# A decoder trunk with product-key experts: 16 tokens of the dense part scored by fetched rows

## The chip, the cores and the metric

One core of one Trainium2 chip runs the whole kernel. The metric is the device time of one execution in microseconds; the number quoted is the median of several runs. The profile and the trace come from one more execution, which has its own time.

## What is computed

One layer of a hybrid decoder for 512 tokens of width 1024: a parallel attention block (sliding-window attention and native sparse attention, merged by gates), a PEER expert layer, a gated per-layer embedding, and a last RMSNorm. The change lies in the PEER layer:

```python
def peer(h, w_q, sub_k1, sub_k2, u, v):        # 16384 experts, 8 heads x 16 picks a token
    ...
    sc, pos = lax.top_k(cand, PEER_TOPK)
    eidx = jnp.take_along_axis(cidx, pos, axis=-1)
    gate = jax.nn.softmax(sc, axis=-1)
    ...
    def chunk_fn(args):
        hx, ex, gx = args
        act = jax.nn.gelu(jnp.einsum('td,thkd->thk', hx, u[ex]))
        return jnp.einsum('thk,thkd->td', (gx.astype(act.dtype) * act), v[ex])
```

Each token picks 128 experts. For each of them the token's row is multiplied with the expert's row of `u`, put through a gelu, weighted by a gate, and used as the weight of the expert's row of `v`.

## The kernel before

The 512 tokens are four tiles of 128. Attention and projections fill the first 540 us. Then the PEER layer is computed in two ways at once.

**Tiles 0 and 1, by fetched rows.** GpSimd issues an indirect DMA per pick (`gather`, L549): it brings, for all 128 tokens of a tile, each token's own row of 1024 floats, 512 KB in all, into one of 8 slots. The `u` rows (n = 0 to 255) are multiplied with the tokens by VectorE (`dot`, L1252, the operation at L1257), then the `v` rows (n = 256 to 511) are weighted and added up (`sum_early`, L1269, and `accumulate`, L1280, the operation at L1292). A fetch waits until the row 8 before it is used (`row_used`), and every consumer waits until its row has landed.

**Tiles 2 and 3, densely, on TensorE.** All 16384 experts go through as 128 chunks of 128. For chunk c, eight matmuls (L1753, 256 token columns each; fp32, so that a matmul is two passes in the trace) give the scores of 256 tokens; ScalarE puts them through the gelu (`dense_activate`, L796). The gates are turned into a matrix of the same shape, four tokens at a time, as a product of two one-hots: `make_hots` on VectorE (L1338), `part_hots` and `gate_hots` on ScalarE (L815, L824), and `mix` on TensorE (L1732, four matmuls of 128 columns). There are 64 such groups, one after each of the score chunks 62 to 125. ScalarE copies the part of a group's product for the chunks still to come (`copy_mix`, L808), VectorE multiplies the chunks already there (`apply_mix`, L1301), and for later chunks it multiplies the gelu with the copied part (`apply_late`, L1309). When the 128 score chunks are done, 128 value chunks follow (`values`, L1764; the operation at L1766), each of four matmuls of 512 columns. The blocks of `u` and `v`, 512 KB a chunk, are streamed by SyncE through a ring of four.

**Who waits for whom.** The orders are written out by hand:

- VectorE takes 134 rows (`EARLY_DOTS`), with the expert search of tiles 1 to 3 between them, then makes the first one-hots. Then there are 65 steps of one-hots, late product, mix product and 2, 2 or 3 rows (`STEP_ROWS`), 151 rows in all. After them the rest of tile 0's `v` rows, then 128 rows of tile 1 with the tail's parts at fixed row numbers (L1396 to L1419).
- TensorE turns the picks of tiles 2 and 3 before chunk 60 (`turn_picks`, L1720). It needs the first one-hots after chunk 62. The tail of tile 0 (the layer embedding and last norm) is placed among the value chunks: `tail_turn(0)` before chunk 80 needs the closed sum of tile 0, and `tail_gate(0)` before chunk 100 (`FIRST_TAIL + 20`, L1774) needs the operand that VectorE makes in `tail_turned(0)` (L1177), placed after its row 42 of tile 1.
- VectorE adds the dense sums of tiles 2 and 3 (`add_dense`, L1220) after its rows 102 and 103 of tile 1. The first waits for tile 2's last value chunk, the second for tile 3's. TensorE's tails of tiles 2 and 3 follow, and the tail of tile 1 comes last, after `close(1)` (L1294).

```python
                if k == 42:
                    tail_turned(0)
                ...
                if c == FIRST_TAIL + 20:
                    tail_gate(0)
                    tail_embed(0)
```

Of the kernel before, what the change touches and what calls it, by code (L numbers as in the profile page):

```python
# [74 lines left out]
EARLY_DOTS = 134  # L75
STEP_ROWS = (2, 2, 3)
# [26 lines left out]
def build(nc, a, out):  # L103
# [4 lines left out]
    with ctx:  # L108
# [14 lines left out]
        pkeys = small[:, 312:568].rearrange("p (h n) -> p h n", h=2)  # L123
        eidx = sb("eidx", [P, NG * COLS], i32)
# [36 lines left out]
        mix_rows = sum(STEP_ROWS[s % len(STEP_ROWS)] for s in range(WG + 1))  # L161
        early_sums = EARLY_DOTS + mix_rows - NG * COLS
        low_slots = NG * COLS + -(-early_sums // SLOTS) * SLOTS
# [79 lines left out]
        assert ha == XS + NG * D  # L243

# [17 lines left out]
        def chunk_scores(c):  # L262
            return ps[6 + c % 2][:, 0:DT]
# [7 lines left out]
        def first_copied(g):  # L271
            return FIRST_MIX + g + 1
# [61 lines left out]
        experts_known = sem("experts_known")  # L334
        row_gathered = [sem(f"row_gathered{b}") for b in range(SLOTS)]
# [191 lines left out]
        def _(pool):  # L527
# [20 lines left out]

            def gather(n):  # L549
                values, k = divmod(n, NG * COLS)  # L550
# [13 lines left out]
                if n >= SLOTS:  # L564
                    pool.wait_ge(row_used, n - SLOTS + 1)
                if low_slots <= n < low_slots + SLOTS and n % SLOTS >= SLOTS - 2:
                    pool.wait_ge(dense_scores, CHUNKS)
                G.indirect_dma_start(out=row_slot(n), out_offset=None, in_=a["v"] if values else a["u"],  # L568
                                     in_offset=bass.IndirectOffsetOnAxis(ap=eidx[:, col:col + 1], axis=0)
                                     ).then_inc(row_gathered[n % SLOTS], 16)  # L570
# [33 lines left out]
            for n in range(2 * NG * COLS):  # L604
                gather(n)
                for t in range(1, TILES):
# [10 lines left out]
        def _(act):  # L617
# [174 lines left out]
            def gelu_dots(t):  # L792
                act.wait_ge(row_used, COLS * (t + 1))
                A.activation(dots[:, t, :], dots[:, t, :], ACT.Gelu_apprx_tanh).then_inc(gelu_ready, 1)

            def dense_activate(c):  # L796
                late = WGRP * groups_before(c)
# [6 lines left out]
                if late < DT:  # L804
                    last = A.activation(mixed[:, c, late:DT], sc[:, late:DT], ACT.Gelu_apprx_tanh)  # L805
# [18 lines left out]
            def gate_hots(g):  # L824
                act.wait_ge(hot2_apart, g + 1)
                for j in range(WGRP):
                    tok = WGRP * g + j
                    last = A.activation(hot2[:, g % 2, j, :], hot2[:, g % 2, j, :], ACT.Relu,  # L828
                                        scale=pickT[:, 3, tok:tok + 1], bias=pickT[:, 2, tok:tok + 1])
                last.then_inc(hot2_gated, 1)  # L830

            for c in range(CHUNKS):
                if c == 8:
                    act.wait_ge(experts_known, 3)
                if c == TURN_AT:
                    act.wait_ge(picks_turned, 2)
# [11 lines left out]
                dense_activate(c)  # L848
                if 0 <= g + 1 < WG:
                    gate_hots(g + 1)  # L850
                if c == 40:
                    gate_exp(2)
# [19 lines left out]
        def _(dve):  # L872
# [379 lines left out]
            def dot(t, k):  # L1252

                n = t * COLS + k
# [14 lines left out]
            def sum_early(k):  # L1269

                n = NG * COLS + k
# [8 lines left out]
            def accumulate(t, k):  # L1280

                n = (NG + t) * COLS + k
# [11 lines left out]
            def close(t):  # L1294
                dve.wait_ge(row_used, (NG + t + 1) * COLS)
# [12 lines left out]

            def apply_late(c):  # L1309
                late = WGRP * groups_before(c)  # L1310
                if late == 0:
                    return
                dve.wait_ge(dense_gelu, c + 1)
                dve.wait_ge(mix_copied, groups_before(c))
                V.tensor_tensor(mixed[:, c, 0:late], mixed[:, c, 0:late], late_gelu[:, c % LATE, 0:late],  # L1315
                                ALU.mult).then_inc(late_applied, 1)
# [21 lines left out]
            def make_hots(g):  # L1338
                if g >= 2:
                    dve.wait_ge(mix_made, g - 1)  # L1340
                V.tensor_tensor(hot1[:, g % 2, :, :], iota[:, :].unsqueeze(1).broadcast_to([P, WGRP, P]),
# [6 lines left out]
            for k in range(EARLY_DOTS):  # L1348
# [15 lines left out]
                if k == EARLY_DOTS - 13:  # L1364
                    gates(2)
                    gates(3)
            def take_row(n):
                if n < NG * COLS:
                    dot(*divmod(n, COLS))
                    return  # L1370
                if n == NG * COLS:
                    weigh(0)
                sum_early(n - NG * COLS)
# [15 lines left out]
            for c in range(FIRST_MIX + WG, CHUNKS):  # L1389
                apply_late(c)  # L1390
# [5 lines left out]
            for k in range(COLS):  # L1396
# [32 lines left out]
        def _(pe):  # L1429
# [290 lines left out]
            def turn_picks():  # L1720
# [9 lines left out]
                last.then_inc(picks_turned, 1)  # L1730

            def mix(g):  # L1732
                pe.wait_ge(hot1_ready, g + 1)
                pe.wait_ge(hot2_gated, g + 1)
                if g < 2:
                    pe.wait_ge(picks_out, 3)
                else:
                    pe.wait_ge(mix_applied, g - 1)
# [133 lines left out]
```

## Time and profile before

| | |
|---|---|
| median of 3 runs | 1641.18 us (1641.04 to 1641.79) |
| the profiled execution, time | 1641.71 us |
| the profiled execution, span of the trace | 1639.9 us |
| TensorE, matmuls | 1608.1 us busy (98%) |
| TensorE, weight loads | 1044.2 us (64%) |
| VectorE | 1043.8 us (64%) |
| GpSimd | 667.2 us (41%) |
| ScalarE | 430.9 us (26%) |
| DMA | 477.70 MB, mean 291 GB/s over the span |
| granted TensorE clock, mean | 0.996 |

The span is the stretch that the trace covers; the time has 1.8 us more around it. Busy time is the time in which an engine has an instruction under way. The granted clock is a share of TensorE's full 2.4 GHz. In the rows, PE is TensorE's matmuls, PEld its weight loads, DVE is VectorE, ACT ScalarE, POOL GpSimd; "arena" is the one large buffer in which most tiles lie, so names tell little and the line numbers count. A bracket behind a timeline row is the idle time before it and who ended it.

### The profile page before, as it was taken

To read this page: it belongs to the slowest core of one execution; us is meant where nothing else is said; L and a number is where in the kernel's file an instruction comes from. 1 tells how busy PE (TensorE), PEld (TensorE's weight loads), DVE (VectorE), ACT (ScalarE), POOL (GpSimd) and SP (SyncE) were. 2 spreads that over 40 slices of the span, in tenths; PEclk is the share of its full clock that TensorE was granted. 3 is DMA by queue.
4 is the path that set the end of the run, shared out by engine and by line. 5 is a ranking of instruction groups with operands and counts; after the bars stand their busy time and mean duration, and the time that the engine had idled before them with its cause. 6 is when DMAs were issued, how large, how long until landed. Compare 5 with 4: busy or idle time off the path is not lost.

```text
span 1639.9 us, 18326 instructions
## 1 busy us (share of the span) xinstructions
PE 1608.1 (98%) x6294; PEld 1044.2 (64%) x6294; DVE 1043.8 (64%) x2380; ACT 430.9 (26%) x1262; POOL 667.2 (41%) x707
## 2 busy tenths in 40 slices
PE   7999999999999999999999999999999999999997
PEld 4446444446786688888899999995444444444443
DVE  2012444432269999999878999996555566667465
ACT  2003444350110211111167777760000000000013
POOL 0002445540001474466745555555433345456340
PEclk9999999999999999999999999999999999999999
DMA  6224111105435899999999999999999999999962
GB/s 232 85 79 148 44 39 39 39 27 167 144 140 175 316 378 401 391 402 397 402 409 408 405 400 408 404 389 406 409 409 409 410 409 406 409 409 409 400 205 91
DMA packets 132698, 477.70 MB, mean 291 GB/s; under 512 B 14796, under 2 KB 15820, under 8 KB 132605
## 3 DMA queue, kind: packets, MB, share of 16 engines
q0 software_dynamic: 73728, 268.47, 41.6%
q1 hardware_dynamic: 58876, 208.06, 34.1%
q8 instruction: 50, 0.82, 0.2%
q14 instruction: 44, 0.35, 0.1%
HBM read 472.24 MB, written 4.24 MB: 291 GB/s over the span
## 4 chain that ended last, share of the span: by engine, by line
PE 93%; DVE 2%; issue 1%; ACT 1%; DMA 1%; POOL 1%; DVEq 0%; SPq 0%
PE psum L1753 27%; PE psum L1766 26%; PE psum L1653 7%; PE psum L1578 6%; PE psum L1454 5%; PE psum L1740 3%; PE psum L1602 3%; PE psum L1614 3%; PE psum L1538 2%; PE psum L1696 2%; PE psum L1553 2%; PE psum L1524 1%; PE psum L1470 1%; PE psum L1638 1%; PE psum L1489 1%
## 5 line engine op out<-in xcount | busy, mean ns | idle before, releaser
L1753 PE MATMUL psum<-arena 128*128 128x256 f32 x2048 | 453.4, 380 | 1.7 <-ACT arena L721 1.7
L1766 PE MATMUL psum<-arena 128*128 128x512 f32 x1024 | 440.3, 593 | 1.7 <-DVE arena L1315 1.1
L1753 PEld LDWEIGHTS psum<-arena 128*128 128x128 f32 x2048 | 384.5, 190 | 51.1 <-issue 2.2
L568 POOL DMA_INDIRECT arena<-in_u,eidx x256 | 257.8, 1007 | 382.7 <-DVE arena L1023 168.2
L568 POOL DMA_INDIRECT arena<-in_v,eidx x256 | 262.2, 1024 | 293.7 <-DVE arena L1292 171.2
L1766 PEld LDWEIGHTS psum<-arena 128*128 128x128 f32 x1024 | 194.6, 190 | 246.1 <-issue 241.3
L1257 DVE CUSTOM_DVE_ANT_0 arena<-psum,arena 128x1024 f32<-128x1024 f32 x256 | 299.9, 1220 | 11.8 <-DMA arena<-in_u,eidx 11.2
L1292 DVE SCALAR_TENSOR_TENSOR arena<-arena,wts 128x1024 f32<-128x1024 f32 x175 | 222.7, 1287 | 106.2 <-DMA arena<-in_v,eidx 106.1
L544 POOL TENSOR_SCALAR arena<-arena 128x256 f32<-128x256 f32 (+4 forms) x128 | 105.9, 846 | 251.3 <-DVE arena L977 191.5
L1578 PE MATMUL psum<-arena 128*128 128x512 f32 x256 | 118.4, 606 | 0.0
L1653 PE MATMUL psum<-arena 128*128 128x256 f32 x512 | 114.7, 384 | 2.4 <-ACT arena L710 2.4
L1653 PEld LDWEIGHTS psum<-arena 128*128 128x128 f32 x512 | 97.6, 193 | 15.8 <-ACT arena L710 3.0
L828 ACT ACTIVATE arena<-arena 128x128 f32<-128x128 f32 x256 | 105.0, 488 | 0.0
L1292 DVE SCALAR_TENSOR_TENSOR psum<-arena,wts,psum 128x1024 f32<-128x1024 f32 x50 | 64.4, 1289 | 49.8 <-DMA arena<-in_v,eidx 49.8
L1454 PE MATMUL psum<-arena 128*128 128x512 f32 x208 | 89.8, 593 | 0.2 <-ACT arena L648 0.2
L805 ACT ACTIVATE arena<-psum 128x256 f32<-128x256 f32 (+31 forms) x126 | 41.3, 328 | 177.3 <-PE psum L1753 176.9
L739 ACT ACTIVATE arena<-arena 128x1024 f32<-128x1024 f32 x4 | 4.2, 1059 | 311.3 <-PE psum L1766 248.0
L820 ACT ACTIVATE arena<-iota,arena 128x128 f32<-128x128 f32 x256 | 81.4, 396 | 0.0
L1578 PEld LDWEIGHTS psum<-arena 128*128 128x128 f32 x256 | 46.1, 190 | 55.4 <-issue 54.4
L686 ACT ACTIVATE arena<-arena 128x256 f32<-128x256 f32 (+4 forms) x128 | 59.8, 469 | 55.2 <-DVE arena L964 44.0
L1454 PEld LDWEIGHTS psum<-arena 128*128 128x128 f32 x208 | 39.4, 190 | 49.3 <-issue 48.6
L1740 PEld LDWEIGHTS psum<-arena 128*128 128x128 f32 x512 | 67.3, 192 | 3.2
(195 smaller groups left out, 1419.8 us busy)
## 6 DMA issues: line engine op xcount, KB each, us to landing
arena<-in_ut SPq DMA_DIRECT2D x128, 512.0 KB, 6.7
arena<-in_vd SPq DMA_DIRECT2D x128, 512.0 KB, 6.9
arena<-in_wpack SPq DMA_DIRECT2D x105, 512.0 KB, 3.6
arena<-in_u,eidx POOLq DMA_INDIRECT x256, 8.8
arena<-in_v,eidx POOLq DMA_INDIRECT x256, 14.7
arena<-in_w_pg SPq DMA_DIRECT2D x8, 512.0 KB, 9.2
arena<-in_x SPq DMA_DIRECT2D x4, 512.0 KB, 5.0
arena<-bias_rows SPq DMA_DIRECT2D x8, 256.0 KB, 5.7
```

Of the source, the lines that this page charges most:

```text
L544: last = G.tensor_scalar(sw[:, i % 3, r, 0:w], sw[:, i % 3, r, 0:w], scl[:, i, r:r + 1], None, ALU.mult)
L568: G.indirect_dma_start(out=row_slot(n), out_offset=None, in_=a["v"] if values else a["u"], in_offset=bass.IndirectOffsetOnAxis(ap=eidx[:, ...
L820: last = A.activation(hot2[:, g % 2, j, :], iota[:, :], ACT.Abs, scale=-1.0, bias=pickT[:, 1, tok:tok + 1])
L828: last = A.activation(hot2[:, g % 2, j, :], hot2[:, g % 2, j, :], ACT.Relu, scale=pickT[:, 3, tok:tok + 1], bias=pickT[:, 2, tok:tok + 1])
L1257: V.tensor_tensor_reduce(out=row_slot(n), in0=dot_rows[t], in1=row_slot(n), scale=1.0, scalar=0.0, op0=ALU.mult, op1=ALU.add, accum_out=do ...
L1292: V.scalar_tensor_tensor(to, row, w, to, ALU.mult, ALU.add).then_inc(row_used, 1)
L1454: last = T.matmul(ps[j % 8], blk(j)[:, k * P:(k + 1) * P], hT[:, k, :], start=(k == 0), stop=(k == KC - 1))
L1578: last = T.matmul(ps[4], blk(B_MG + m)[:, k * P:(k + 1) * P], hT[:, k, :], start=(k == 0), stop=(k == KC - 1))
L1653: last = T.matmul(ps[4 + p % 2][:, jj * HT:(jj + 1) * HT], blk(b)[:, k * P:(k + 1) * P], h2T[:, k, :], start=(k == 0), stop=(k == KC - 1))
L1740: last = T.matmul(mix_bank(g)[:, j * P:(j + 1) * P], hot1[:, g % 2, j, :], hot2[:, g % 2, j, :], start=True, stop=True)
L1753: last = T.matmul(chunk_scores(c), u[:, k * P:(k + 1) * P], h2T1[:, k, :], start=(k == 0), stop=(k == KC - 1))
L1766: last = T.matmul(ps[VALUE_BANK[t] + h], mixed[:, c, t * P:(t + 1) * P], stream[:, c % SRING, h * HALF:(h + 1) * HALF], start=(c == 0), st ...
```

## The change

The last 16 tokens of tile 3 leave the dense scores, which then have 240 columns. Their 128 picks each are spread over the 128 partitions as 8 parts of 16 picks (16 tokens x 8 parts), so that 16 more fetched `u` rows serve all of them (n = 176 to 191). TensorE makes the spread token rows with matmuls against an identity (`mid_rows`) and the spread picks and gates with two more matmuls; VectorE makes the dot products (`mid_dot`), ScalarE the gelu, and the weights are turned back by one small matmul in chunk 98. For the last four groups the weight is multiplied into the first one-hot, and the mix product is copied whole, with no gelu to multiply it with. Besides, `apply_late` goes from VectorE's queue to GpSimd's, between the fetches; VectorE takes 136 early rows and then 2, 2, 2, 2 or 3 a step; and the dense tiles are added ten rows earlier.

```diff
-EARLY_DOTS = 134
-STEP_ROWS = (2, 2, 3)
+EARLY_DOTS = 136
+STEP_ROWS = (2, 2, 2, 2, 3)
+MID = 16
+MID_PARTS = P // MID
+MID_AT = 176
+MID_GELU = FIRST_MIX + 30
+MID_BACK = FIRST_MIX + 36
+DN = DT - MID
+MID_FIRST = DN // WGRP
...
+        u_rows = NG * COLS + MID
+        early_sums = rows_taken(WG + 1) - u_rows
...
         def chunk_scores(c):
-            return ps[6 + c % 2][:, 0:DT]
+            return ps[6 + c % 2][:, 0:DN]
...
-            for n in range(2 * NG * COLS):
+            def apply_late(c):
+                late = WGRP * late_groups(c)
+                if late == 0:
+                    return
+                pool.wait_ge(dense_gelu, c + 1)
+                pool.wait_ge(mix_copied, late_groups(c))
+                G.tensor_tensor(mixed[:, c, 0:late], mixed[:, c, 0:late], late_gelu[:, c % LATE, 0:late],
+                                ALU.mult).then_inc(late_applied, 1)
+
+            for n in range(2 * NG * COLS + MID):
                 gather(n)
+                for step in range(1, WG + 1):
+                    if n == rows_taken(step) + SLOTS - 1:
+                        apply_late(FIRST_MIX + step - 1)
+                        if step == WG:
+                            for c in range(FIRST_MIX + WG, CHUNKS):
+                                apply_late(c)
...
+            def widen():
+                act.wait_ge(rows_stashed, 16 * TILES)
+                A.activation(token_wide.rearrange("p (q c) -> p q c", c=MID),
+                             ident[:, P - MID:P].unsqueeze(1).broadcast_to([P, MID_PARTS, MID]), ACT.Copy).then_inc(mid_wide_ready, 1)
+                for k in range(KC):
+                    last = A.activation(h_wide[k // 4][:, k % 4, :].rearrange("p (q c) -> p q c", c=MID),
+                                        h2T1[:, k, DN:DT].unsqueeze(1).broadcast_to([P, MID_PARTS, MID]), ACT.Copy)
...
             for c in range(CHUNKS):
+                if c == 48:
+                    widen()
...
             make_hots(0)
+            spread_picks()
             taken = EARLY_DOTS
             for s in range(WG + 1):
-                if s + 1 < WG:
+                if 1 <= s < WG - 1:
                     make_hots(s + 1)
-                if s >= 1:
-                    apply_late(FIRST_MIX + s - 1)
+                if 1 <= s <= MID_FIRST:
                     apply_mix(s - 1)
+                if s == MID_GELU - FIRST_MIX + 3:
+                    weigh_mid()
                 more = STEP_ROWS[s % len(STEP_ROWS)]
                 for n in range(taken, taken + more):
                     take_row(n)
                 taken += more
-            for c in range(FIRST_MIX + WG, CHUNKS):
-                apply_late(c)
+                if s == 0:
+                    dve.wait_ge(mid_rows_made, 1)
+                    make_hots(1)
+            dve.wait_ge(mix_copied, WG)
...
-                if k == 102:
+                if k == 92:
                     add_dense(2)
-                if k == 103:
+                if k == 93:
                     add_dense(3)
                     tail_scale(1)
-                if k == 105:
+                if k == 95:
                     tail_turned(1)
                     tail_scale(2)
-                if k == 106:
+                if k == 96:
                     tail_turned(2)
...
+                pe.wait_ge(mid_wide_ready, 3)
+                T.matmul(ps[5][:, DT:DT + P], token_wide, esel.rearrange("p h k -> p (h k)"), start=True, stop=True)
+                T.matmul(ps[5][:, DT + P:DT + 2 * P], token_wide, gateD[:, 1, :], start=True,
+                         stop=True).then_inc(picks_turned, 1)
+
+            def mid_rows():
+                pe.wait_ge(row_used, COLS)
+                for k in range(KC):
+                    last = T.matmul(ps[k // 4][:, (k % 4) * P:(k % 4 + 1) * P],
+                                    h_wide[k // 4][:, k % 4, :], ident[:, :], start=True, stop=True)
+                last.then_inc(mid_rows_made, 1)
...
                 for k in range(KC):
-                    last = T.matmul(chunk_scores(c), u[:, k * P:(k + 1) * P], h2T1[:, k, :], start=(k == 0), stop=(k == KC - 1))
+                    last = T.matmul(chunk_scores(c), u[:, k * P:(k + 1) * P], h2T1[:, k, 0:DN], start=(k == 0), stop=(k == KC - 1))
+                if c == MID_BACK:
+                    pe.wait_ge(mid_weighed, 1)
+                    last = T.matmul(ps[6 + c % 2][:, DT:DT + MID], mid_wide, mid_same_token, start=True, stop=True)
                 last.then_inc(dense_scores, 1)
+                if c == TURN_AT + 1:
+                    mid_rows()
```

The new reductions on VectorE, right behind the first one-hots:

```diff
+            def spread_picks():
+                apart = [P, 2, MID_PARTS, MID]
+                V.tensor_reduce(mid_same_part, ident[:, :].rearrange("p (q c) -> p q c", c=MID), AX.X, ALU.add)
+                after(V.tensor_reduce(mid_same_token, ident[:, :].rearrange("p (q c) -> p c q", c=MID), AX.X, ALU.add))
+                V.tensor_tensor(mid_pick.rearrange("p a (q c) -> p a q c", c=MID),
+                                ps[5][:, DT:2 * DT].rearrange("p (a q c) -> p a q c", a=2, c=MID),
+                                mid_same_part.unsqueeze(1).unsqueeze(3).broadcast_to(apart), ALU.mult).then_inc(mid_spread, 1)
```

## Rows read from the trace of the kernel before

**Rows 1.** The chain that ended last, shares by engine.

```profile
PE 93%; DVE 2%; issue 1%; ACT 1%; DMA 1%; POOL 1%; DVEq 0%; SPq 0%
```

**Rows 2.** Windows by stage: us, busy us (count) per engine, clock, DMA share, GB/s.

```profile
617.00:833.00 216.00, 215.23 (x1001) 189.72 (x1002) 197.82 (x618) 38.34 (x90) 127.06 (x141) 1.00 1.01 399
833.00:1114.00 281.00, 281.00 (x1550) 254.51 (x1549) 259.03 (x460) 208.10 (x693) 151.78 (x149) 1.00 1.02 402
1116.00:1545.00 429.00, 428.43 (x1005) 190.23 (x1004) 264.08 (x213) 8.11 (x11) 206.71 (x202) 1.00 1.03 409
```

**Rows 3.** The chain in order of time: start us, us, engine, line, count.

```profile
548.05 15.77 PE psum L1653 x64
564.71 6.91 PE psum L1653 x32
617.77 204.05 PE psum L1753 x944
...
822.48 10.36 PE psum L1753 x48
833.73 3.46 PE psum L1753 x16
...
1107.57 6.92 PE psum L1753 x32
1115.61 268.05 PE psum L1766 x624
...
1460.90 13.73 PE psum L1696 x32
```

**Rows 4.** VectorE's waits from 612 to 830 us: us, times, longest.

```profile
DVE arena L1257 <- DMA arena<-in_u,eidx: 9.8, 10, 2.7
```

**Rows 5.** Timeline of VectorE before the mix: start us, us, instruction, idle before.

```profile
825.26 1.23 DVE L1257 CUSTOM_DVE_ANT_0 arena<-psum,arena 128x1024 f32<-128x1024 f32 x1 [1.54 <-DMA arena<-in_u,eidx]
826.41 1.29 DVE L1341 TENSOR_TENSOR arena<-iota,arena 128x512 f32<-128x512 f32 x2
...
833.77 0.69 DVE L1341 TENSOR_TENSOR arena<-iota,arena 128x512 f32<-128x512 f32 x1 [3.65 <-PE psum L1740]
```

**Rows 6.** Timeline of TensorE around 544 us.

```profile
543.66 1.06 PE L1627 MATMUL psum<-ident,arena 128*128 128x128 f32 x8 [2.27 <-DVE arena L1036]
```

**Rows 7.** Window of 2 us behind that gap, columns as in rows 2.

```profile
546.00:548.00 2.00, 1.18 (x6) 0.77 (x4) 1.93 (x3) 2.00 (x4) 0.00 (x0) 0.50 0.73 297
```

**Rows 8.** Timeline of VectorE late in the mix stage.

```profile
1109.74 0.41 DVE L1315 TENSOR_TENSOR arena<-arena,late_gelu 128x252 f32<-128x252 f32 x1
1110.07 0.67 DVE L1306 TENSOR_TENSOR arena<-arena,psum 128x504 f32<-128x504 f32 x1
1110.66 2.67 DVE L1278 SCALAR_TENSOR_TENSOR psum<-arena,wts,psum 128x1024 f32<-128x1024 f32 x2
```

**Rows 9.** Lines 601 and 1128: ns min/median/max, first and last start us.

```profile
L601 POOL TENSOR_TENSOR arena<-arena x18: 1443/1745/1762, 576.0 to 794.1; 128x800 f32<-128x800 f32 x12, 128x640 f32<-128x640 f32 x6
L1128 DVE TENSOR_TENSOR arena<-candno,arena x18: 818/992/2510, 574.2 to 786.5; 128x800 f32<-128x800 f32 x12, 128x640 f32<-128x640 f32 x6
```

**Rows 10.** Timeline of VectorE: turn of tile 0, and the end.

```profile
1430.59 1.28 DVE L1180 TENSOR_TENSOR arena<-psum,small 128x512 f32<-128x512 f32 x2
...
1543.27 1.29 DVE L1292 SCALAR_TENSOR_TENSOR arena<-arena,wts 128x1024 f32<-128x1024 f32 x1 [1.45 <-DMA arena<-in_v,eidx]
1567.44 1.28 DVE L1228 TENSOR_TENSOR arena<-arena,psum 128x512 f32<-128x512 f32 x2 [22.89 <-PE psum L1766]
...
1574.24 1.29 DVE L1228 TENSOR_TENSOR arena<-arena,psum 128x512 f32<-128x512 f32 x2 [4.32 <-PE psum L1766]
...
1581.76 16.04 DVE L1292 SCALAR_TENSOR_TENSOR arena<-arena,wts 128x1024 f32<-128x1024 f32 x13
...
1611.28 1.23 DVE L1299 TENSOR_TENSOR arena<-arena 128x1024 f32<-128x1024 f32 x1
```

**Rows 11.** Timeline of TensorE: tail gates of tiles 2 and 3.

```profile
1582.65 27.63 PE L1696 MATMUL psum<-arena 128*128 128x512 f32 x64
```

More of the change, by code:

```diff
@@ L160, in build, with rows_taken, u_row @@
         assert SL + (SLOTS - 2) * D <= XS
-        mix_rows = sum(STEP_ROWS[s % len(STEP_ROWS)] for s in range(WG + 1))
-        early_sums = EARLY_DOTS + mix_rows - NG * COLS
-        low_slots = NG * COLS + -(-early_sums // SLOTS) * SLOTS
+        def rows_taken(step):
+            return EARLY_DOTS + sum(STEP_ROWS[s % len(STEP_ROWS)] for s in range(step))
+        u_rows = NG * COLS + MID
+        early_sums = rows_taken(WG + 1) - u_rows
+        low_slots = u_rows + -(-early_sums // SLOTS) * SLOTS
+        def u_row(i):
+            return i if i < MID_AT else i + MID
         vslots = slots[:SLOTS - 2] + [place(H2 + i * D, [D])[0] for i in range(2)]
@@ L334, in build @@
         experts_known = sem("experts_known")
+        mid_wide_ready = sem("mid_wide_ready")
+        mid_spread = sem("mid_spread")
+        mid_known = sem("mid_known")
+        mid_rows_made = sem("mid_rows_made")
+        mid_gelu = sem("mid_gelu")
+        mid_weighed = sem("mid_weighed")
+        mid_weights_out = sem("mid_weights_out")
         row_gathered = [sem(f"row_gathered{b}") for b in range(SLOTS)]
@@ L546, in _, with fetch @@
                 last.then_inc(probs_ready, 1)
-            def gather(n):
-                values, k = divmod(n, NG * COLS)
+            def fetch(n, table, picks):
+                if n >= SLOTS:
+                    pool.wait_ge(row_used, n - SLOTS + 1)
+                if low_slots <= n < low_slots + SLOTS and n % SLOTS >= SLOTS - 2:
+                    pool.wait_ge(dense_scores, CHUNKS)
+                G.indirect_dma_start(out=row_slot(n), out_offset=None, in_=table,
+                                     in_offset=bass.IndirectOffsetOnAxis(ap=picks, axis=0)
+                                     ).then_inc(row_gathered[n % SLOTS], 16)
+            def gather(n):
+                if MID_AT <= n < MID_AT + MID:
+                    c = n - MID_AT
+                    if c == 0:
+                        pool.wait_ge(mid_known, 1)
+                    fetch(n, a["u"], mid_idx[:, c:c + 1])
+                    return
+                values, k = divmod(n - MID if n >= MID_AT else n, NG * COLS)
                 col = k // COLS * COLS + PICK_ORDER[k % COLS]
@@ L563, in gather @@
                     pool.wait_ge(rows_normed, 2 * TILES)
[L564 to L570, printed above, removed]
+                fetch(n, a["v"] if values else a["u"], eidx[:, col:col + 1])
             def number_pairs(t):
@@ L803, in dense_activate @@
                     last = A.activation(late_gelu[:, c % LATE, 0:late], sc[:, 0:late], ACT.Gelu_apprx_tanh)
-                if late < DT:
-                    last = A.activation(mixed[:, c, late:DT], sc[:, late:DT], ACT.Gelu_apprx_tanh)
+                if late < DN:
+                    last = A.activation(mixed[:, c, late:DN], sc[:, late:DN], ACT.Gelu_apprx_tanh)
                 last.then_inc(dense_gelu, 1)
@@ L1340, in make_hots @@
                     dve.wait_ge(mix_made, g - 1)
+                if g >= MID_FIRST:
+                    dve.wait_ge(mid_weights_out, 1)
+                    for j in range(WGRP):
+                        tok = WGRP * g + j
+                        last = V.tensor_scalar(hot1[:, g % 2, j, :], iota[:, :], pickT[:, 0, tok:tok + 1],
+                                               pickT[:, 2, tok:tok + 1], ALU.is_equal, ALU.mult)
+                    last.then_inc(hot1_ready, 1)
+                    return
                 V.tensor_tensor(hot1[:, g % 2, :, :], iota[:, :].unsqueeze(1).broadcast_to([P, WGRP, P]),
@@ L1736, in mix @@
                     pe.wait_ge(picks_out, 3)
+                    pe.wait_ge(mid_spread, 1)
+                elif g - 2 < MID_FIRST:
+                    pe.wait_ge(mix_applied, g - 1)
                 else:
-                    pe.wait_ge(mix_applied, g - 1)
+                    pe.wait_ge(mix_copied, g - 1)
                 for j in range(WGRP):
```

82 lines of the change are left out of this document (59 added, 23 removed).

## The prediction, made before the result

> **What bounds the kernel now.** I read the chain that ended last first: TensorE holds 93% of it, the dense scores (L1753) and the dense values (L1766) over half [rows 1]. Then the windows by stage [rows 2]: TensorE is busy throughout from 617 us on, but the DMA column matters as much. It stands at 399 GB/s beside the first scores, at 402 in the mix stage and at 409, its ceiling here, beside the values. So two flows run side by side: TensorE, and the fetched rows that VectorE consumes at the DMA's pace. Wherever TensorE waits for a row, the second flow sets the time.
>
> TensorE's steps [rows 3]: a score chunk takes 3.457 us (16 passes of 256 columns, 0.216 us each); a mix step is 4.347 us, so its four matmuls (8 passes of 128 columns) add 0.89 us, 0.111 us a pass. The scores end at 1114.5, the values begin at 1115.6, and at 1460.9 TensorE goes into the first tail gate (L1696), which follows value chunk 99.
>
> **Part 1: 240 columns in place of 256.** Between 0.111 us at 128 columns and 0.216 us at 256, a straight line gives 0.203 us at 240: 0.21 us less per chunk, 27 us over 128 chunks. The lower bound of the gain is zero, if the weight loads hold the pace; I take the line, since the loads already keep up with 0.111 us a pass in the mix. The new TensorE work before the mix, eight matmuls for the wide rows and two for the picks (20 passes of 128 columns), is 2.2 us; the back-turn of the weights is under 0.1 us. ScalarE's nine widening copies lie beside chunks in which it is used 38 us of 216 [rows 2]: nothing.
>
> **Part 2: before the mix, 62 chunks, 13 us of that gain.** TensorE would be ready for the first mix at 832.8 - 13.0 + 2.2 = 822. But this mix needs the first one-hots, which VectorE makes only after its early dots. Their last rows came late from the DMA: VectorE waited 9.8 us for rows in this stage [rows 4], 1.54 us just before the last early dot at 825.3, and made the one-hots at 826.4 [rows 5]. Now there are two more early dots (136), the streamed blocks come 6% faster and take that from the rows, and the new reductions stand ahead of the mix. VectorE's own work would let it be there at about 818 (826.4 less its waits, plus 2.3); the DMA's supply says 829 to 832 for the last row, then 0.7 us of one-hots and 1 us of spreading. I take 832.0 for the first mix, near the DMA's end, as the stage already moved 399 of 409 GB/s. So TensorE idles about 10 us there, and **12 of the 13 us are gone**. It also comes back slow: after the 2.27 us gap before 543.7 [rows 6] the granted clock fell to 0.50, the lower level (1.2 GHz) [rows 7], and 64 passes took 15.77 us where 32 take 6.91 soon after [rows 3]: 2.0 us lost.
> The Trainium skill, page "TensorE: Matmul & The Clock Gate" (section "What's actually happening"), has an idle array throttled to half rate; by that, too, the idle time costs more than itself. The trace agrees (0.50).
>
> **Part 3: the mix stage, 65 chunks.** TensorE gains 65 x 0.21 = 13.7 us. VectorE has per step one-hots 0.6, the mix product up to 0.67, and now 2.2 rows at 1.15 (dots) or 1.33 (sums) [rows 5, 8], 3.8 us with dots, under the new step of 4.14. Its late products (0.41 at 252 wide [rows 8]) go to GpSimd: by the 640-wide product there, 1.44 us [rows 9], some 0.6 us each, three of them at the end with 0.3 us more before the values. GpSimd is used 152 of 281 us [rows 2], so they fit; they wait for a chunk's gelu and mix copy, and behind them in the same queue stand the row fetches, which have 8 slots of lead. The DMA needs 512 KB per 4.14 us of stream and 2.2 rows: 406 GB/s, just under 409. So the scores end at 1114.5 - 0.8 - 13.7 + 2.0 = 1102.0 and the values begin at 1103.4, **12 us earlier**.
>
> **Part 4: the debt of rows.** By the end of the mix VectorE had taken 134 + 151 = 285 rows; now it has taken 136 + 143 = 279, 16 of which are new. So 22 more rows are left for the values stage. Which wait ends last there? The first tail gate needs the turned tile 0, and VectorE turns it after row 42 of tile 1 (L1400), a place the change leaves alone. Before, that was done at 1431.9 [rows 10], 29 us ahead of TensorE (1460.9). From 1113.3 [rows 8] it took 142 rows; now it must take 121 + 43 = 164. At 409 GB/s a 512 KB row costs 1.28 us, and a streamed block every 3.43 us leaves one row per 2.04 us: 22 rows are 45 us. From about 1100, the turn comes at 1100 + 317 + 45 = 1462, while TensorE is at chunk 100 at 1103.4 + 345.3 = 1448.7. Once TensorE stands and its four blocks are in, rows come at 1.28 us, which saves 2.5; the two turning operations add 1.3. So **TensorE stands about 12 us, until 1461**, and again loses 2.0 us to the low clock. The values end at 1461 + (1574.2 - 1460.9) + 2.0 = 1576.3: 2 us later than before. The bounds of this term: 4 us with the rows 10 us earlier (all the DMA's idle share before 1114 used), 18 us with the rows at the mix's old pace.
>
> **Part 5: the end.** The dense tiles are added at rows 92 and 93 in place of 102 and 103. VectorE already sat 22.9 us before the first of them, waiting for the values [rows 10]; at row 92 it sits there again, about 16 us by the same row count. After the values, 34 rows are left and not 24. From 1574.2 to 1612.4 VectorE is busy without a gap with 24 rows and the tail's parts [rows 10]; 13 rows take 16.04 us with their overlap, 1.19 each beyond the first, so ten more are 11.9 us: 50.1 us. They were covered once by TensorE's tail for tiles 2 and 3 (done at 1610.3, 2.3 us before tile 1's [rows 11]); the cover is used up, so all of it counts. Tile 1's tail stays 27.5 us, plus 0.7 (my estimate, a third of the 2.0 above) for a TensorE that now comes back from a longer idle time.
>
> **Sum**, against the profiled execution (span 1639.9, time 1641.7, so 1.8 around it): 1576.3 + 50.1 + 27.5 + 0.7 = 1654.6, and 1.8 makes 1656.4. The median shown is 0.5 lower: **1656 us**, 0.9% slower.
>
> **Rivals.**
> A (the forecast, 0.66): TensorE waits for row 42. Bounds 1643 to 1664.
> B (faster, 0.12): the rows keep up; neither wait arises, since gathers find unused DMA time and VectorE's own work ends by 818. Then 27 - 2.5 = 24.5 us stay: values end at 1549.7, and + 50.1 + 27.5 + 0.7 + 1.8 gives 1630. It decides if row 42's turn is done by 1437, 24 us ahead of my count. Against it: 409 GB/s at every window from 1116 on.
> C (no change, 0.10): the wait before the mix arises, that at the first tail gate doesn't (turn done by 1449): values end at 1562, total 1642. For it: the slack was 29 us; against it, 22 rows are 45 us.
> D (slower still, 0.12): the mix stage does not shrink, from either of two causes with one price: 240 columns save nothing, or GpSimd's products hold up VectorE. The trace has such a case: the 800-wide comparison on VectorE takes 0.99 us alone and up to 2.51 beside GpSimd's products [rows 9]. If a product of 0.6 us were added whole to VectorE's 3.8, its step would be 4.4, past 4.14. All 13.7 us would be lost: 1670. Against it: VectorE gives up its own late product.
> The Trainium skill, page "SBUF — State Buffer" (section "SBUF: two separate sides"), has VectorE operations with two SBUF inputs and GpSimd operations that read SBUF block each other whole; by it D's second cause holds for the one-hots, and the times of that comparison agree (0.99 and 2.51). The early dots read one input from PSUM, so by that rule they go free.
>
> **Numbers.** 0.2% (3.3 us) is about what a measurement of this kernel can tell from no change. Faster is B and a sliver of A, 0.13; same is C and A's edge, 0.11; slower 0.76. The range goes from 1641, which takes in C's 1642 and leaves out B, to 1668, short of D's full price.
>
> **What would show it.** Per step: a score chunk at 3.25 us on the chain; TensorE idle some 10 us before the first mix product, released by VectorE, with a granted clock of 0.5 behind it; the mix steps at 4.14; 279 rows taken when the values begin at about 1103; TensorE idle some 12 us before the first L1696 matmul, released by the turn of tile 0; VectorE idle before the dense add at row 92; 50 us from the last value to the last sum; GpSimd's products under 0.8 us. The forecast is wrong if the turn comes before TensorE asks for it, which needs rows faster than one per 2.04 us beside the stream, or if over 279 rows are taken by then; and its size is wrong if the mix steps stay at 4.35.

## The result and the profile after

The changed kernel takes **1662.4 us** (median of 4 runs, 1660.0 to 1663.2), beside 1641.1 (1637.4 to 1641.8) for the kernel before: 1.0132 times as long, interval 1.0113 to 1.0151. The forecast was 1656, with 1641 to 1668 as its range. On another chip the same file gave 1.0118 (1.0103 to 1.0134). The profiled execution took 1661.7 us, span 1659.9, so the same 1.8 us lie around it, and the sum of the prediction (span 1654.6) stands against 1659.9.

First the windows of the changed kernel, columns as in [rows 2]:

```profile
617.00:833.00 216.00, 204.44 (x1018) 191.08 (x1018) 199.37 (x617) 41.20 (x103) 126.88 (x142) 0.99 1.02 403
833.00:1114.00 281.00, 277.67 (x1572) 259.94 (x1573) 249.96 (x431) 204.94 (x688) 179.32 (x213) 0.99 1.02 403
1116.00:1545.00 429.00, 415.06 (x967) 183.62 (x966) 268.27 (x215) 8.11 (x11) 202.38 (x207) 0.98 1.03 409
```

TensorE, busy throughout before [rows 2], now has holes: 12 us in the first window, 14 in the last. The DMA is at 403 and 409 GB/s, where it was at 399 and 409: it was full, and it is full. What ended TensorE's holes is in its list of waits (us in total, times, longest):

```profile
PE psum L1798 <- DVE arena L1378: 14.7, 1, 14.7
PE psum L1807 <- DVE arena L1259: 13.6, 1, 13.6
PE psum L1865 <- DVE small L1449: 9.3, 1, 9.3
...
PE psum L1835 <- DVE arena L1243: 3.5, 1, 3.5
```

All four are releases by VectorE. The last two lie before the mix: `turn_picks` (L1835) waits for the dense gates and the first mix product (L1865) for the new reductions (L1449). The second is the first tail gate (L1807) waiting for the turned tile 0 (L1259). The first is tile 1's own turn, after the last row, where nothing else is left for TensorE.

Where the stages stand in TensorE's time (chain of waits; start us, us, line, count), as in [rows 3]:

```profile
834.89 2.04 PE psum L1865 x8
836.94 4.00 PE psum L1878 x16
840.94 0.89 PE psum L1865 x8
845.07 0.89 PE psum L1865 x8
```

The mix begins at 834.9. Its first eight passes take 2.04 us where later ones take 0.89, and the first chunk behind them 4.00 against 3.24: about 1.9 us lost to the low clock (a granted clock of 0.50 until 838.3 us, 1.00 from there on). From then on a step is 4.13 us (840.94 to 845.07), against 4.35 before [rows 3]. The other end, the turn of tile 0 in VectorE's timeline, and then TensorE's (start us, us, instruction, idle before):

```profile
1463.46 1.28 DVE L1259 TENSOR_TENSOR arena<-psum,small 128x512 f32<-128x512 f32 x2
```

```profile
1464.88 16.42 PE L1807 MATMUL psum<-arena 128*128 128x512 f32 x32 [13.57 <-DVE arena L1259]
1481.14 3.60 PE L1823 MATMUL psum<-arena 128*128 128x512 f32 x8
1484.58 96.30 PE L1897 MATMUL psum<-arena 128*128 128x512 f32 x224
1580.71 3.60 PE L1823 MATMUL psum<-arena 128*128 128x512 f32 x8
```

TensorE came to this gate at 1451.3, 9.6 us earlier than before (1460.9 [rows 3]), stood 13.57 us, and took 16.42 us for the 32 matmuls that took 13.73 (at a granted clock of 0.50 until 1469.8). So it left the gate 6.7 us later than before (1481.1, where it was 1474.5), and the value matmuls end 6.7 us later too. VectorE's timeline after them:

```profile
1574.11 1.29 DVE L1307 TENSOR_TENSOR arena<-arena,psum 128x512 f32<-128x512 f32 x2 [24.71 <-PE psum L1897]
...
1580.91 1.28 DVE L1307 TENSOR_TENSOR arena<-arena,psum 128x512 f32<-128x512 f32 x2 [4.32 <-PE psum L1897]
...
1588.43 28.44 DVE L1371 SCALAR_TENSOR_TENSOR arena<-arena,wts 128x1024 f32<-128x1024 f32 x23
...
1630.36 1.22 DVE L1378 TENSOR_TENSOR arena<-arena 128x1024 f32<-128x1024 f32 x1
```

VectorE sits 24.7 us at row 92 for the dense sums, and then has 23 rows in one block where it had 13 [rows 10]. From the second dense sum to the end of tile 1's sum (1580.9 to 1631.5) it takes 50.6 us, against 38.2 before.

### The profile page after: what moved, and what is told of

It is laid out like the page before. It is cut to its first block, busy times and chain, and to the rows that moved or that the text cites. A ratio compares the mean times of both kernels' runs of the same rounds, so it can differ in the third digit from the quotient of the medians.

```text
span 1659.9 us, 18445 instructions
## 1 busy us (share of the span) xinstructions
PE 1589.3 (96%) x6316; PEld 1048.2 (63%) x6316; DVE 1057.0 (64%) x2362; ACT 430.2 (26%) x1269; POOL 701.8 (42%) x788
## 2 busy tenths in 40 slices
DMA packets 135001, 486.09 MB, mean 293 GB/s; under 512 B 15051, under 2 KB 16075, under 8 KB 134908
## 4 chain that ended last, share of the span: by engine, by line
PE 53%; DMA 24%; DVE 14%; issue 4%; POOL 4%; ACT 1%; DVEq 0%; SPq 0%; POOLq 0%
DMA arena<-in_v,eidx 19%; PE psum L1878 11%; PE psum L1689 6%; PE psum L1897 6%; PE psum L1565 5%; DVE arena L1336 5%; DMA arena<-in_u,eidx 4%; PE psum L1764 3%; PE psum L1713 3%; PE psum L1725 3%; PE psum L1865 3%; PE psum L1649 2%; PE psum L1807 2%; POOL arena L587 2%; PE psum L1664 2%
## 5 line engine op out<-in xcount | busy, mean ns | idle before, releaser
L1878 PE MATMUL psum<-arena 128*128 128x240 f32 x2048 | 427.2, 367 | 1.7 <-ACT arena L778 1.7
L1878 PEld LDWEIGHTS psum<-arena 128*128 128x128 f32 x2048 | 384.5, 190 | 26.4 <-issue 2.4
L587 POOL DMA_INDIRECT arena<-in_v,eidx x256 | 252.6, 987 | 279.4 <-DVE arena L1371 173.6
L1897 PEld LDWEIGHTS psum<-arena 128*128 128x128 f32 x1024 | 194.3, 190 | 246.4 <-issue 243.5
L1371 DVE SCALAR_TENSOR_TENSOR arena<-arena,wts 128x1024 f32<-128x1024 f32 x186 | 236.1, 1290 | 110.3 <-DMA arena<-in_v,eidx 110.2
L1764 PE MATMUL psum<-arena 128*128 128x256 f32 x512 | 114.8, 383 | 2.4 <-ACT arena L767 2.4
L1371 DVE SCALAR_TENSOR_TENSOR psum<-arena,wts,psum 128x1024 f32<-128x1024 f32 x61 | 78.6, 1289 | 56.0 <-DMA arena<-in_v,eidx 55.9
L1764 PEld LDWEIGHTS psum<-arena 128*128 128x128 f32 x512 | 97.4, 193 | 16.0 <-ACT arena L767 3.0
L886 ACT ACTIVATE arena<-arena 128x128 f32<-128x128 f32 x240 | 98.4, 488 | 1.4 <-PE psum L1850 1.4
L862 ACT ACTIVATE arena<-psum 128x240 f32<-128x240 f32 (+29 forms) x122 | 39.0, 320 | 163.4 <-PE psum L1878 163.3
L1689 PEld LDWEIGHTS psum<-arena 128*128 128x128 f32 x256 | 46.0, 189 | 55.5 <-issue 54.4
L1865 PE MATMUL psum<-arena 128*128 128x128 f32 x512 | 68.5, 277 | 9.3 <-DVE small L1449 9.3
L1865 PEld LDWEIGHTS psum<-arena 128*128 128x128 f32 x512 | 67.9, 194 | 11.2 <-issue 9.6
## 6 DMA issues: line engine op xcount, KB each, us to landing
arena<-in_v,eidx POOLq DMA_INDIRECT x256, 14.7
```

Source lines behind the costliest of these rows:

```text
L587: G.indirect_dma_start(out=row_slot(n), out_offset=None, in_=table, in_offset=bass.IndirectOffsetOnAxis(ap=picks, axis=0)).then_inc(row_ga ...
L1371: V.scalar_tensor_tensor(to, row, w, to, ALU.mult, ALU.add).then_inc(row_used, 1)
L1689: last = T.matmul(ps[4], blk(B_MG + m)[:, k * P:(k + 1) * P], hT[:, k, :], start=(k == 0), stop=(k == KC - 1))
L1764: last = T.matmul(ps[4 + p % 2][:, jj * HT:(jj + 1) * HT], blk(b)[:, k * P:(k + 1) * P], h2T[:, k, :], start=(k == 0), stop=(k == KC - 1))
L1865: last = T.matmul(mix_bank(g)[:, j * P:(j + 1) * P], hot1[:, g % 2, j, :], hot2[:, g % 2, j, :], start=True, stop=True)
L1878: last = T.matmul(chunk_scores(c), u[:, k * P:(k + 1) * P], h2T1[:, k, 0:DN], start=(k == 0), stop=(k == KC - 1))
```

## The experiments

Twelve runs on four more chips, numbered 2 to 5 here. The kernel before was timed on each. The chips are of two kinds. On chips 4 and 5 it takes 1641.5 and 1641.2 us, as on the first chip. On chips 2 and 3 it takes 1652.0 and 1650.7, and on them the change costs much more, in a way told below. So ratios are compared only between chips of one kind. One more variant, with 128 early dots in place of 136, gave no time. So what the wait before the first mix costs by itself was not measured.

### The changed kernel again

On a chip of each kind. 

> The changed kernel itself once more, as the measure for the three beside it, since the chip of the last call gave the kernel before 1652 and not 1641 us, and showed engines standing for 10 to 27 us with no semaphore behind it. Debt of rows: 1.3% over the kernel before, on whatever chip. Rival (the chip of the last call, not the edits, made e1, e4 and e5 slow): on such a chip the changed kernel is itself 50 us over the kernel before; on one like the first it is 20 us over.

Measured (chip 3, second kind): 1708.0 us (1701.1 to 1719.0), ratio 1.0337 (1.0303 to 1.0370).

> The changed kernel itself, unedited, beside the runs of this call. On the first chip its ratio to the kernel before was 1.013; on the two chips after it 1.034, with about 48 us lost around the first tail gate. If the loss there belongs to the chip, this one comes out near one of the two values, and the others of this call are read against it.

Measured (chip 4, first kind): 1660.8 us, ratio 1.0118 (1.0103 to 1.0134). Its trace repeats the one above: 13.45 us at the gate, 9.9 before the mix.

### Tile 0 turned after row 26

```diff
-                if k == 42:
+                if k == 26:
                     tail_turned(0)
```

> The changed kernel with the turn of tile 0 after row 26 of tile 1 in place of row 42, nothing else. Debt of rows: the turn is done 16 x 2.04 = 33 us earlier, near 1432, before TensorE asks at 1451; the 13.6 us wait and its 2.7 us of half clock go, the values end at 1565 and not 1581; VectorE reaches row 92 at about 1560, some 2 us late for the first dense add, so 14 to 16 us less: 1646 to 1648 us. Rival (the wait at the gate only covers another one, and TensorE stands as long elsewhere): within 3 us of 1662.

> The turn of tile 0 after row 26 again, beside the changed kernel. Debt of rows: the 13.6 us at the first tail gate and its half clock go, 14 to 16 us under it, so 0.3 to 0.4% over the kernel before. Rival: TensorE stands as long elsewhere, within 3 us of it.

Measured (chips 2 and 3, second kind): 1.0044 (1.0020 to 1.0067) and 1.0034 (1.0011 to 1.0057). Against 1.0337 for the changed kernel on chip 3, one number moved in VectorE's order takes away 48 us, where 14 to 16 were expected. The wait at L1807 is gone from TensorE's list, as forecast. But 14 us of standing can't be 48; what else went is the subject of the section on hardware.

### The dense tiles added at row 102 again

```diff
-                if k == 92:
+                if k == 102:
                     add_dense(2)
```

(and 93, 95, 96 back to 103, 105, 106)

> The changed kernel with one part undone: the dense tiles are added at rows 102, 103, 105 and 106 of tile 1 again. Debt of rows (the theory: the time is set by the rows that VectorE still has to take when TensorE asks for something behind them): VectorE sat 24.7 us before row 92's dense add, long enough for ten more rows, so 24 and not 34 rows follow the last value; 10 x 1.19 = 11.9 us less, 1650 us; TensorE still stands some 14 us at the first tail gate. Rival (the time is lost before the mix and to GpSimd's products, the order at the end is hidden): 1662 us, as the change.

> The dense add at rows 102, 103, 105, 106 again, beside the changed kernel. Debt of rows: 10 to 12 us under it (24 and not 34 rows behind the last value). Rival (order at the end hidden): the same time as it. If the earlier 1709 us came from the edit, it is 45 us over it.

Measured (chips 2 and 3, second kind): 1.0330 (1.0274 to 1.0387) and 1.0362 (1.0328 to 1.0396), no gain beside 1.0337. The runs of one kernel scatter by 5 to 18 us there, so a gain of 12 is hard to settle on those chips by the time alone. The traces do show a shorter end: from the start of the matmuls behind the last value to the end of the span it is 79.5 us in the changed kernel, and 65.8 and 65.7 in these two. Hence a third run, on the other kind:

> The changed kernel with the dense tiles added at row 102 again and nothing else, on another chip. Where SyncE keeps issuing blocks (values end near 1581 us), the 10 rows moved ahead of the end of the value matmuls should take 12 us off: ratio 1.005 in place of 1.012, and VectorE waits about 10 us for the last value matmuls in place of 25. If the ratio stays at 1.012, the rows after the values were not what set the end. If SyncE stops here too, values end near 1638 and the ratio is about 1.034.

Measured (chip 5, first kind): 1647.7 us, ratio **1.0036** (1.0024 to 1.0048), against 1.0118 and 1.0132 of the changed kernel. VectorE's timeline:

```profile
1576.70 1.28 DVE L1307 TENSOR_TENSOR arena<-arena,psum 128x512 f32<-128x512 f32 x2 [6.91 <-PE psum L1897]
...
1583.49 1.28 DVE L1307 TENSOR_TENSOR arena<-arena,psum 128x512 f32<-128x512 f32 x2 [4.32 <-PE psum L1897]
...
1591.02 16.03 DVE L1371 SCALAR_TENSOR_TENSOR arena<-arena,wts 128x1024 f32<-128x1024 f32 x13
...
1620.53 1.22 DVE L1378 TENSOR_TENSOR arena<-arena 128x1024 f32<-128x1024 f32 x1
```

The value matmuls end 2.6 us later than in the changed kernel, and still the kernel is 13 us faster: 6.9 us of idle time where 24.7 were, and 38.2 us from the second dense sum (1583.5) to the end of tile 1's (1621.7), 12.4 fewer than the 50.6 above. The tail behind it is 2.7 us shorter too (25.7 for 28.4): TensorE stood 14.7 us before it in the changed kernel, and 2.3 here. 12.4 + 2.7 - 2.6 = 12.5, the difference of the spans (1659.9 and 1647.4). That settles Part 5, for the case in which TensorE stands at the gate: the ten rows on the far side of the values count in full.

### The same late turn in the kernel before

```diff
-                if k == 42:
+                if k == 68:
                     tail_turned(0)
```

> The kernel before, with tile 0 turned for its gate after row 68 in place of row 42 and nothing else: TensorE should stand at the first gate as long as in the changed kernel (26 rows at 1.8 us put the turn near 1475 us, where TensorE asks at 1461: 12 to 14 us), and its next matmuls at half clock (2 to 3 us). If a stand at that gate is enough to stop the stream of value blocks, the ratio is 1.028 to 1.034 on a chip where c1_changed is at 1.034. If the stop needs something else of the change, the ratio is 1.008 to 1.010, the stand alone.

Measured (chip 4, first kind): 1662.4 us, ratio **1.0127** (1.0112 to 1.0143), as much as the whole change loses, with nothing of the change in it. That the sizes agree is chance: the stand is longer here, and the end is not touched. TensorE's timeline:

```profile
1479.74 17.01 PE L1696 MATMUL psum<-arena 128*128 128x512 f32 x32 [19.82 <-DVE arena L1180]
1496.59 3.60 PE L1712 MATMUL psum<-arena 128*128 128x512 f32 x8
1500.03 96.30 PE L1766 MATMUL psum<-arena 128*128 128x512 f32 x224
1596.16 3.60 PE L1712 MATMUL psum<-arena 128*128 128x512 f32 x8
```

The stand came out at 19.8 us, not 12 to 14: the 26 rows took 47.7 us (1430.6 to 1478.3), 1.8 each as assumed, which my sum should have put at 1477 and not at 1475. And 17.01 for the 32 matmuls is 3.3 more than 13.73. Together they are 23.1, of which 20.9 us arrive in the time. So in this kernel a stand at this gate is paid nearly in full. The chip was of the kind on which the blocks keep coming, so the other half of the question was not answered.

### Both cures, and a smaller change

The turn at row 26 and the dense sums at 102 in the changed kernel:

> Both cures in the changed kernel: tile 0 turned after row 26 and the dense tiles added at row 102. If 10 rows less after the value matmuls are worth 12 us by themselves, the ratio is 0.996. If VectorE, once TensorE no longer stands, reaches row 92 only as the value matmuls end (in the run with the turn at row 26 it waited 0.25 us there), the place of the dense sums decides nothing, and the ratio is that of the turn alone, 1.003 to 1.004.

Measured (chip 4): 1642.2 us, ratio **1.0008** (0.9999 to 1.0017), no difference from the kernel before, and neither of the two expected values (0.996, and 1.003 to 1.004). TensorE stands nowhere in the values stage for more than 1.3 us (timelines of TensorE, then of VectorE):

```profile
1450.47 13.90 PE L1807 MATMUL psum<-arena 128*128 128x512 f32 x32
...
1565.74 3.60 PE L1823 MATMUL psum<-arena 128*128 128x512 f32 x8
1573.91 1.97 PE L1798 MATMUL psum<-ident,arena 128*128 128x128 f32 x8 [4.58 <-DVE arena L1307]
```

```profile
1563.69 8.97 DVE L1371 SCALAR_TENSOR_TENSOR arena<-arena,wts 128x1024 f32<-128x1024 f32 x7 [0.28 <-DMA arena<-in_v,eidx]
1572.58 1.28 DVE L1307 TENSOR_TENSOR arena<-arena,psum 128x512 f32<-128x512 f32 x2
1574.97 1.28 DVE L1307 TENSOR_TENSOR arena<-arena,psum 128x512 f32<-128x512 f32 x2
```

TensorE is through with the values 8.3 us ahead of the kernel before (the matmuls behind them start at 1565.7, where they started at 1574.0). It gains nothing by it: VectorE reaches row 102 only at 1572.6, with no idle time left ahead of the dense sums, and adds the second one at 1575.0, where the kernel before did so at 1574.2 [rows 10]. The rows set the end now, and 16 more of them are what the 240 columns were bought with. They have used up the 22.9 us that VectorE waited there in the kernel before [rows 10].

The same with 8 tokens taken out in place of 16:

```diff
-MID = 16
+MID = 8
```

> The change with 8 tokens in place of 16 (score matmuls 248 wide, 8 more u rows), the turn at row 26 and the dense tiles at row 102. If the rows that VectorE and the DMA have to carry set the end once the stand at the gate is gone, 8 rows less are worth 8 x 1.24 us = 10 us against the run with both cures, and the wider matmuls cost nothing: ratio 0.997. If TensorE's columns set it, 8 more columns cost 4 to 7 us and the ratio is 1.006 to 1.008.

Measured (chip 4): 1637.8 us, ratio **0.9984** (0.9975 to 0.9993): 3.7 us under the kernel before, the fastest file of the study, though by less than the 0.2% that I called measurable. The wait before the first mix is 2.6 us, and the second dense sum follows TensorE (timeline of VectorE):

```profile
1566.99 1.28 DVE L1307 TENSOR_TENSOR arena<-arena,psum 128x512 f32<-128x512 f32 x2
1570.67 1.29 DVE L1307 TENSOR_TENSOR arena<-arena,psum 128x512 f32<-128x512 f32 x2 [1.20 <-PE psum L1897]
```

Here both flows end within 2 us of each other. Against the run with both cures 4.4 us are won where 10 were expected, since TensorE, with wider matmuls, is now the one that ends last.

### The two things that were doubted

The late products back on VectorE, and 256 columns again:

```diff
                 if s >= 1:
+                    apply_late(FIRST_MIX + s - 1)
...
-                    last = T.matmul(chunk_scores(c), u[:, k * P:(k + 1) * P], h2T1[:, k, 0:DN], ...
+                    last = T.matmul(chunk_scores(c), u[:, k * P:(k + 1) * P], h2T1[:, k, :], ...
```

> The changed kernel with the late products back on VectorE, as before the change; all else as changed. Debt of rows: VectorE's step grows from 3.8 to 4.2 us at most, about TensorE's 4.13; the rows taken by the end of the mix stay 279; within 3 us of 1662. Rival (GpSimd's products hold VectorE or the fetches up): faster than 1662 by 5 us or more, with the 2.9 us that the scores ended later than forecast gone.

> The changed kernel with the score matmuls 256 columns wide again (16 of them unused), all else as changed: it takes the gain in columns away alone. Debt of rows: before the first mix TensorE's 13 us were idle time anyway, so it is ready at about 835 and nothing is lost there; the mix stage is 13.7 us longer, less 2 us of half clock that goes with the wait; rows and turn shift with it, so about 1662 + 12 = 1674 us, with no wait before the first mix and the one at the tail gate as long as now. Rivals: 1689 if all 27 us of columns count; 1662 if none do.

Measured (chip 2, second kind): 1.0328 (1.0279 to 1.0376) for the late products on VectorE, beside 1.0337 for the changed kernel on chip 3. The step of the mix is 4.13 us in both, so that part of the change does nothing to the step; an effect of a few us on the time would not show on these chips. For 256 columns 1.0421 (1.0373 to 1.0469). On the chain a chunk is 3.46 us again and a step 4.35:

```profile
951.24 3.46 PE psum L1878 x16
955.59 3.46 PE psum L1878 x16
959.94 3.46 PE psum L1878 x16
```

The 16 columns are worth about 0.8% there, 14 us: the 14 of the mix stage, not the 27 of all chunks. Between two chips that scatter so, that is a size and not a proof. The trace adds something that the time doesn't show. The scores end 12.4 us later than in the changed kernel on chip 3, the gate opens 13.2 us later (1493.0 for 1479.8), and TensorE stands there as long as ever, 13.5 us. So a later end of the mix moves the rows along with TensorE.

## Why the prediction was right, and where it was short

The forecast was rival A, and it is what happened: both waits arise, where they were expected, and the rows behind the values count. The kernel is 1.3% slower, where 0.9% was forecast; 5.3 us of span are missing from the sum.

- **Part 1, 240 columns.** 0.203 us a pass was taken, and 3.24 us a chunk makes 0.2025. The gain of 27 us is there, chunk by chunk; ScalarE's copies cost nothing that shows.
- **Part 2, before the mix.** Forecast: first mix at 832.0. Measured: 834.9. The last early dot did come late from the DMA (the chain has 12.37 us of `u` row fetches up to 832.0). I took the DMA's last row between 829 and 832, and it was the end of that span; I also left out the dot itself, 1.15 us between the row and the one-hots, which start at 833.1. One-hots and the spread then took 1.8 us, where 1.7 were summed. All 13 us of the stage's gain are gone, and 2 more (the first mix began at 832.8 before). The low clock took 1.9 us, forecast 2.0.
- **Part 3, the mix stage.** Forecast: 4.14 us a step, scores end at 1102.0, values from 1103.4. Measured: 4.13, 1104.8, 1106.2; the 2.8 us are those of Part 2. GpSimd's products have a median of 0.48 us (0.21 to 0.72), forecast 0.6. Rival D, that the stage does not shrink, is refuted, and the run with the products on VectorE shows that it needed no relief either.
The Trainium skill, page "SBUF — State Buffer" (section "SBUF: two separate sides"), makes GpSimd operations that read SBUF and VectorE operations with two SBUF inputs exclude each other. The trace gave that rule no occasion. Of the 60 one-hot operations of the stage only one overlaps a product, by 0.01 us, and all take 0.68 to 0.69 us. The products fell beside dots and mix products, which read PSUM. Besides, VectorE had time to spare: it waited 23.6 us in this stage for ScalarE.
- **Part 4, the debt of 22 rows.** Forecast: the turn done at 1461, a stand of 12 us, 2.0 us of low clock, values end at 1576.3. Measured: 1464.9, 13.6, 2.7, 1580.9. So 3.9 + 0.7 = 4.6 of the 5.3 us appear here, but the count of rows was right and most of the 3.9 came from Part 2. VectorE's last row of the mix stage ended at 1102.9, not at "about 1100", as late as the mix itself was:

```profile
1094.66 8.27 DVE L1357 SCALAR_TENSOR_TENSOR psum<-arena,wts,psum 128x1024 f32<-128x1024 f32 x6
```

From there the turn took 361.8 us, where 361 were reckoned. In the changed kernel on chip 3 the scores ended 15.0 us later than on the first chip, and the gate opened 14.9 us later. So what was mis-sized is the moment of the first mix in Part 2. It delayed TensorE (to the gate by 2.6 us) and the rows (by 2.9) alike, and that is why the stand came out near the forecast. The cause of the stand can be read more simply too. Counted by VectorE's row operations, 425 rows were done by 1430 us, and 426 in the kernel before. The rows came at the same pace by the clock. The turn now stands 16 rows further on, and was done 32.9 us later (1464.7 for 1431.9): 2.05 us a row, where the prediction had 2.04.
- **Part 5, the end.** Forecast 50.1 + 27.5 + 0.7, measured 50.6 and 28.4. The idle time ahead of row 92 was 24.7 us, not "about 16": 4.6 of it is the later end of the values, and the rest were rows that came faster than I let them while TensorE stood and no blocks were streamed beside them. VectorE takes 19 rows in one block of 23.48 us right behind the turn (from 1464.7 on), where they had come about 2 us apart. It ran ahead, to wait longer.

What I had not seen is how the two late places add up. I had the gate and the tail as two costs of one change. The runs have the tail at 13 to 15 us (dense sums at 102: 1647.7 against 1660.8 and 1662.4), and the two together at 19 to 20 us (both cures: 1642.2 against the same). So the gate is worth 5.5 us once the tail is right: the end then passes from TensorE to the rows. (The early turn alone was not run on the first kind of chip.) Of the 27 us that TensorE saved, none is left even so. 16 more rows of 512 KB are 8.4 MB, which the page shows (486.09 MB against 477.70), and at 409 GB/s that is 20.5 us of a DMA that has none to give from 617 us on.

## What to carry to other kernels

Taking work from the busiest engine pays only up to the resource that runs beside it. TensorE was at 93% of the chain here, but the DMA was at 399 to 409 of 409 GB/s in the same stages, and a trade of matmul columns for fetched rows was one of 27 us against 20. When rows are added to a flow that others wait for at fixed row numbers, those numbers are part of the change: recount for each such place when it comes, and put it where both sides meet.

## What the runs showed of the hardware

**On two of five chips SyncE stops issuing blocks.** On the second kind of chip the stand at the gate was the same 13.57 us, yet it set off something else. TensorE's timeline in the changed kernel, chip 3:

```profile
1479.75 15.57 PE L1807 MATMUL psum<-arena 128*128 128x512 f32 x32 [13.57 <-DVE arena L1259]
1495.16 3.60 PE L1823 MATMUL psum<-arena 128*128 128x512 f32 x8
1498.59 13.90 PE L1897 MATMUL psum<-arena 128*128 128x512 f32 x32
1537.65 5.34 PE L1897 MATMUL psum<-arena 128*128 128x512 f32 x8 [25.17 <-issue]
1555.86 82.01 PE L1897 MATMUL psum<-arena 128*128 128x512 f32 x184 [12.86 <-DMA arena<-in_vd]
```

Four chunks after the gate, as many as the ring holds, it runs dry for 25.17 us, and 12.86 us more a little later: 38 us, and 52 with the gate's own 14, beside the 48 that the early turn saved. The waits of SyncE's queue, on this chip from 1440 to 1600 us, then on the first one from 1450 to 1560 (us in total, times, longest):

```profile
SPq L529 <- remote: 85.0, 3, 64.4
SPq L529 <- PE psum L1897: 61.6, 18, 9.0
```

```profile
SPq L529 <- PE psum L1897: 101.4, 22, 36.5
```

On the first chip the longest pause in the stream is 36.5 us, and TensorE ends it by freeing a block. Here it is 64.4 us, 28 more, and nothing that the profile records ends it ("remote"). Meanwhile the DMA is not idle; its queues in the window from 1480 to 1530 us (packets, MB, share of 16 engines):

```profile
q0 software_dynamic: 5601, 20.39, 102.5%
q8 instruction: 1, 0.02, 0.1%
q14 instruction: 2, 0.02, 0.1%
```

Only fetched rows move, 39 of them, at full rate, and VectorE takes them and then idles 84.5 us at row 92. The Trainium skill, page "DMA: Bandwidth & Descriptors" (section "Queues, rings and completion order"), has each DMA engine take turns between its queues. The trace doesn't contradict it: SyncE issued no block between 1466.2 and 1530.9, so there was nothing in its queue to take a turn. What held SyncE is open. ScalarE shows the same kind of wait on these chips ahead of the mix (timeline of ScalarE):

```profile
814.69 0.37 ACT L862 ACTIVATE arena<-psum 128x240 f32<-128x240 f32 x1 [7.96 <-remote]
833.12 0.63 ACT L862 ACTIVATE arena<-psum 128x240 f32<-128x240 f32 x2 [18.06 <-remote]
```

From 815 to 833 us, too, nearly all that moved were fetched rows (95.3% on the software queue, one block issued). Instruction packets share these DMA engines; that an engine waits there for its own instructions is a guess that fits, and no run tested it. What is shown is that on these chips the long hold comes with the stand. In the five runs that had the stand, SyncE issued no block for 62 to 75 us from about the gate on. In the two with the turn at row 26 the longest pause there was 20.6 us, as long as in the kernel before on the first chip, and no wait was put down to "remote" between 1400 and 1600 us (elsewhere there were some, at most 20.3 us). With the dense sums at 102 alone the hold stayed. Whether the kernel before would suffer it too, given the same stand, is open: that was only run on a chip of the first kind.

**A stand costs more than its length.** Nine runs had a stand at the gate, of 12.7 to 19.8 us. The 32 matmuls behind it took 15.57 to 17.05 us in place of 13.73: 1.8 to 3.3 us more. They began at a granted clock of 0.50, and the longer that lasted behind the stand, the more it cost: 3.2 us where they took 15.57, 4.9 us where they took 16.42, and 6.1 us where they took 17.01.
